# Decoder trunk: two pieces of the second modulation chunk as 128-column products on TensorE, the forget columns fetched from ScalarE's queue, the first weight units asked for sooner

## The reference, cut to what matters

```
cond = silu(c)                                  # 2048 numbers
mod  = cond @ w_mod[l] + b_mod[l]               # 2048 x 12288 weights a layer
sh1, sc1, g1, sh2, sc2, g2 = split(mod, 6)
h    = rms_norm(x, gain) * (1 + sc1) + sh1
proj = h @ w_attn_in                            # q, k, v and eight forget columns
...                                             # attention, output projection, MLP; layer 2 with pooling
```

## Time and profile before

| | us |
|---|---|
| median of 3 executions | 2059.95 (2057.93 to 2060.64) |
| the profiled execution's own time | 2060.63 |
| its span, first to last instruction | 2059.0 |
| TensorE busy in the span | 1987.6 (97%) |
| VectorE busy | 1661.6 (81%) |
| ScalarE busy | 1058.5 (51%) |
| GpSimd busy | 271.1 (13%) |

### The profile page before, as it was taken

How to read it: one execution, slowest core, us unless ns; L and a number is a source line. 1 busy time by engine, 2 the same in 40 slices (tenths; PEclk the granted TensorE clock), 3 DMA queues, 4 the chain that set the end, 5 groups by cost and what they waited for, 6 DMA issues and landing times.

```text
span 2059.0 us, 29840 instructions
## 1 busy us (share of the span) xinstructions
PE 1987.6 (97%) x10792; PEld 1711.1 (83%) x10792; DVE 1661.6 (81%) x2185; ACT 1058.5 (51%) x1556; POOL 271.1 (13%) x459
## 2 busy tenths in 40 slices
PE   3999999998999999999999999899999999999998
PEld 2878989887888888888888887688888888888886
DVE  5777899897899999999989977889965666566665
ACT  4323764554655544565446565565543555434553
POOL 3242342220111111111111100011000000000000
PEclk8999999999999999999999999999999999999999
DMA  9999899896789999998999874397756555555552
GB/s 361 356 357 324 308 333 333 301 321 216 270 311 326 315 375 349 323 331 313 353 367 322 312 260 155 110 321 266 263 193 198 184 187 195 191 191 195 187 185 101
DMA packets 235984, 558.99 MB, mean 271 GB/s; under 512 B 14040, under 2 KB 15048, under 8 KB 235336
## 3 DMA queue, kind: packets, MB, share of 16 engines
q1 hardware_dynamic: 180552, 355.81, 50.0%
q0 software_dynamic: 55296, 201.35, 27.5%
HBM read 555.02 MB, written 2.10 MB: 271 GB/s over the span
## 4 chain that ended last, share of the span: by engine, by line
PE 78%; DVE 10%; issue 5%; DMA 4%; ACT 2%; POOL 0%; DVEq 0%; POOLq 0%; ACTq 0%
PE ps L767 28%; PE ps L772 14%; PE ps L791 8%; PE ps L793 8%; PE ps L792 8%; DVE w_lo L1561 4%; PE ps L811 3%; DMA mraw<-in_w_mod 3%; PE ps L742 2%; PE ps L743 2%; PE ps L744 2%; PE ps L808 1%; DVE macc L1590 1%; DVE macc L1575 1%; ACT work L1186 1%
## 5 line engine op out<-in xcount | busy, mean ns | idle before, releaser
L1186 ACT ACTIVATE w_hi<-raw 128x1024 fp32r<-128x1024 f32 x640 | 670.9, 1057 | 742.1 <-PE ps L767 261.9
L1561 DVE TENSOR_TENSOR w_lo<-raw,w_hi 128x1024 fp32r<-128x1024 f32 x640 | 766.9, 1224 | 273.2 <-ACT w_hi L1186 272.4
L767 PE MATMUL ps<-h_pair,w_hi 128*128 128x512 f32 x2816 | 684.6, 393 | 7.9 <-DVE w_lo L1561 5.9
L767 PEld LDWEIGHTS ps<-h_pair,w_hi 128*128 128x128 f32 x2816 | 515.2, 188 | 115.7 <-issue 16.3
L772 PEld LDWEIGHTS ps<-h_pair,w_lo 128*128 128x128 f32 x2816 | 360.9, 191 | 14.0
L772 PE MATMUL ps<-h_pair,w_lo 128*128 128x256 f32 x2816 | 365.1, 283 | 0.0
L791 PE MATMUL ps<-w_hi,g_hi 128*128 128x512 f32 x832 | 327.5, 394 | 0.8 <-DVE w_lo L1561 0.6
L793 PE MATMUL ps<-w_hi,g_lo 128*128 128x512 f32 x832 | 324.0, 389 | 0.0
L792 PE MATMUL ps<-w_lo,g_hi 128*128 128x512 f32 x832 | 323.8, 389 | 0.0
L1590 DVE SCALAR_TENSOR_TENSOR macc<-mraw,cond,macc 128x1024 f32<-128x1024 f32 x180 | 230.5, 1282 | 29.1 <-DMA mraw<-in_w_mod 21.2
L1575 DVE SCALAR_TENSOR_TENSOR macc<-mraw,cond,macc 128x512 f32<-128x512 f32 x284 | 196.0, 747 | 30.7 <-DMA mraw<-in_w_mod 22.9
(11 more groups left out here) (182 smaller groups left out, 1571.2 us busy)
## 6 DMA issues: line engine op xcount, KB each, us to landing
mraw<-in_w_mod POOLq DMA_DIRECT2D x358, 512.0 KB, 6.3
raw<-in_w_up SPq DMA_DIRECT2D x176, 1024.0 KB, 6.1
raw<-in_w_down SPq DMA_DIRECT2D x88, 1024.0 KB, 5.9
raw<-in_w_attn_in SPq DMA_DIRECT2D x48, 1024.0 KB, 8.9
raw<-in_w_attn_out SPq DMA_DIRECT2D x16, 1024.0 KB, 7.4
work<-in_w_mod POOLq DMA_DIRECT2D x12, 512.0 KB, 8.7
early<-in_w_mod POOLq DMA_DIRECT2D x8, 512.0 KB, 12.5
raw<-in_w_pool SPq DMA_DIRECT2D x4, 1024.0 KB, 5.2
```

The costliest lines, as they stand in the source:

```text
L767: i = mm(ps[:, bank + t, :], w_hi[:, s, kk, t * P:(t + 1) * P], h_pair[:, k, :, :].rearrange("p a t -> p (a t)"), start=first and half == ...
L1186: return nc.scalar.activation(o, i, f, **kw)
L1561: V.tensor_tensor(w_lo[:, s, :, :], raw[:, j % 4, h * 1024:(h + 1) * 1024].rearrange("p (k n) -> p k n", k=2), w_hi[:, s, :, :].bitcast(F3 ...
```

## The change

It has five parts.

1. Pieces 6 and 7 of chunk 1 leave VectorE (4 of its 14 operations). TensorE multiplies them instead (`seed_product`): the piece's 128 x 128 blocks stand still and a column of `cond`, repeated 128 times, moves, so the products both scale the rows and sum them over the partitions. Piece 6 comes first, then the accumulator of VectorE against 128 columns of ones, then piece 7, all into PSUM bank 3. `mod_bias` of chunk 1 reads every 128th column there.
2. SP asks for units 0 to 3 when `mod_acc` reaches 14, 19, 22 and 32. Chunk 1 adds only 10 of its 14 counts by products; the other 4 are added after its last addition.
3. `bfb` is issued by SP right behind the parameters. `wf` is issued by ScalarE, behind the four copies of the first quarter of `h`.
4. TensorE runs `mod_sum` of chunk 0 ahead of the transposes of x, and the transposes of the parameters behind the first two of the eight groups of x. ScalarE copies in that order.
5. VectorE's `mod_bias` of chunk 0 moves behind the last addition of chunk 1; those of chunks 2, 4 and 6 move ahead of the last piece of the chunk that follows.

```diff
@@ -344,6 +344,8 @@
+        SEEDS = (6, 7)
+        X_BANKS = (0, 1, 2, 0, 1, 2, 4, 5)
...
@@ -494,10 +496,13 @@
                     sp.dma_start(prow[0:FT2, CWcol(l, i):CWcol(l, i) + P], rows(conv_w[l, i])).then_inc(s_prm, 16)
                 sp.dma_start(prow[0:FT2, CBcol(l):CBcol(l) + P], rows(conv_b[l])).then_inc(s_prm, 16)
+            with nc.allow_non_contiguous_dma("the forget bias on every partition"):
+                sp.dma_start(bfb[:, :], b_forget[0:1, :].to_broadcast([P, NF])).then_inc(s_wf, 16)
             def load(q, j, src):
                 if isinstance(q, int) and q == 0:
-                    sp.wait_ge(mod_acc, (22, 24, 26, 34)[j])
+                    sp.wait_ge(mod_acc, (14, 19, 22, 32)[j])
                     if j >= 2:
...
@@ -514,11 +519,6 @@
                              src.rearrange("(k p) n -> p k n", p=P)).then_inc(raw_landed[j % 4], 16)
             for pos in range(48):
-                if pos == 4:
-                    with nc.allow_non_contiguous_dma("the eight forget columns, the bias on every partition"):
-                        sp.dma_start(wf[:, :, :], w_attn_in[0, :, 3 * D:3 * D + NF]
-                                     .rearrange("(k p) n -> p k n", p=P)).then_inc(s_wf, 16)
-                        sp.dma_start(bfb[:, :], b_forget[0:1, :].to_broadcast([P, NF])).then_inc(s_wf, 16)
                 hg, kind, ks = qkv_unit(pos)
...
@@ -830,6 +830,26 @@
                            start=True, stop=True)
                 i.then_inc(mod_red, 1)
+            def seed_product(j):
+                pe.wait_ge(early_landed[j], 16)
+                for kk in range(2):
+                    for t in range(4):
+                        i = mm(ps[:, 3, t * P:(t + 1) * P], mod_slot(1, j)[:, kk, t * P:(t + 1) * P],
+                               cond[:, 2 * j + kk:2 * j + kk + 1].to_broadcast([P, P]),
+                               start=j == SEEDS[0] and kk == 0 and t == 0,
+                               stop=j == SEEDS[1] and kk == 1, skip_group_check=True)
+                return i
+            def seeded_sum():
+                seed_product(SEEDS[0])
+                pe.wait_ge(mod_added, 2)
+                for t in range(4):
+                    mm(ps[:, 3, t * P:(t + 1) * P], macc[:, 0, 0, t * P:(t + 1) * P], ones[:, :],
+                       start=False, stop=False, skip_group_check=True)
+                seed_product(SEEDS[1]).then_inc(mod_red, 1)
...
@@ -892,26 +912,35 @@
             pe.wait_ge(consts, C_IDENT)
             pe.wait_ge(s_c, 16)
             nc.tensor.transpose(ps[:, 7, 0:KT], prow[0:KT, 0:P], ident[0:KT, 0:KT]).then_inc(c_t, 1)
-            pe.wait_ge(xn0_ready, 2)
-            for b in range(8):
-                if b >= 4:
-                    pe.wait_ge(x_copied, b - 3)
+            def turn_x(b):
+                if 3 <= b < 6:
+                    pe.wait_ge(x_copied, b - 2)
+                elif b >= 6:
+                    pe.wait_ge(prm_ready, b - 5)
                 for t in range(2):
                     for a in range(QT):
                         k = 2 * b + t
-                        i = nc.tensor.transpose(ps[:, b % 4, (2 * t + a) * P:(2 * t + a + 1) * P],
+                        i = nc.tensor.transpose(ps[:, X_BANKS[b], (2 * t + a) * P:(2 * t + a + 1) * P],
                                                 xn_first[:, a, k * P:(k + 1) * P], ident[:, :])
                 i.then_inc(x_t, 1)
+            pe.wait_ge(consts, C_ONES)
+            pe.wait_ge(cond_s, 1)
+            pe.wait_ge(xn0_ready, 1)
+            mod_sum(0, 1, 0)
+            pe.wait_ge(xn0_ready, 2)
+            turn_x(0)
+            turn_x(1)
             pe.wait_ge(s_prm, 16 * (3 + 5 * LAYERS))
             for b in range(11):
                 i = nc.tensor.transpose(ps[:, 4 + b // 4, (b % 4) * P:(b % 4) * P + ROWS[b]],
                                         prow[0:ROWS[b], b * P:(b + 1) * P], ident[0:ROWS[b], 0:ROWS[b]])
                 if b in (3, 7, 10):
                     i.then_inc(prm_t, 1)
-            pe.wait_ge(prm_ready, 3)
-            pe.wait_ge(consts, C_ONES)
-            pe.wait_ge(cond_s, 1)
-            mod_sum(0, 1, 0)
+            for b in range(2, 8):
+                turn_x(b)
...
@@ -1045,9 +1074,12 @@
                     mod_sum(3, 0, 0)
-            mod_sum(1, 0, 0)
-            pe.wait_ge(x_copied, 8)
+            seeded_sum()
+            pe.wait_ge(x_copied, 6)
+            pe.wait_ge(prm_ready, 3)
             for pos in range(POS0):
+                if pos == 1:
+                    pe.wait_ge(x_copied, 8)
                 start_unit(pos)
...
@@ -1290,6 +1329,10 @@
             for cq in range(3):
                 first_products(2 * cq + 2, 1, 2 * cq + 1)
                 modulate(0, range(4 * cq, 4 * cq + 4))
+                if cq == 0:
+                    with nc.allow_non_contiguous_dma("the eight forget columns"):
+                        act.dma_start(wf[:, :, :], w_attn_in[0, :, 3 * D:3 * D + NF]
+                                      .rearrange("(k p) n -> p k n", p=P)).then_inc(s_wf, 16)
                 if cq < 2:
                     part_copy(6 * cq)
...
@@ -1564,7 +1607,8 @@
             def piece(c_all, j, a):
-                if j:
+                seeded = isinstance(c_all, int) and c_all == 1
+                if j and not (seeded and j in SEEDS):
                     dve.wait_ge(*mod_landing(c_all, j))
                     for kk in range(2):
                         k = 2 * j + kk
@@ -1575,9 +1619,11 @@
                         V.scalar_tensor_tensor(macc[:, a, kk, :], mod_slot(c_all, j)[:, kk, :], cond[:, k:k + 1],
                                                macc[:, a, kk, :], ALU.mult, ALU.add).then_inc(mod_acc, 1)
                 if j == 7:
-                    dve.wait_ge(mod_acc, 14 * since(c_all) + 14)
+                    dve.wait_ge(mod_acc, 14 * since(c_all) + (14 - 2 * len(SEEDS) if seeded else 14))
                     V.tensor_tensor(macc[:, a, 0, :], macc[:, a, 0, :], macc[:, a, 1, :],
                                     ALU.add).then_inc(mod_added, 1)
+                    if seeded:
+                        dve.sem_inc(mod_acc, 2 * len(SEEDS))
...
@@ -1715,8 +1764,10 @@
                         norm_stats(0)
                     if ch == 0 and j == 6:
                         norm_rstd(0)
-                    if ch == 1 and j == 6:
+                    if ch == 1 and j == 7:
                         dve.wait_ge(prm_ready, 3)
+                        mod_bias(ch - 1, 0, first_chunk(ch - 1))
+                    if ch > 1 and ch % 2 and j == 6:
                         mod_bias(ch - 1, 0, first_chunk(ch - 1))
                     if ch >= 2:
                         if ch % 2 == 0 and j == 1:
@@ -1728,8 +1779,6 @@
                             part_add(first + ((0, 6), (1, 2), (1, 5)).index((ch % 2, j)))
                 if ch % 2:
                     cq = ch // 2
-                    if ch > 1:
-                        mod_bias(ch - 1, 0, first_chunk(ch - 1))
                     mod_bias(ch, 0, first_chunk(ch))
                     norm_gain_vec(0, 4 * cq, 4 * cq + 4)
                     for t in range(4 * cq, 4 * cq + 4):
```

More of the change, by code:

```diff
@@ L1265, in _, with x_copy @@
             first_products(1, 0, None)
-            for b in range(8):
+            def x_copy(b):
                 act.wait_ge(x_t, b + 1)
-                A(xnT[:, 2 * b:2 * b + 2, :].rearrange("p a n -> p (a n)"), ps[:, b % 4, :],
+                A(xnT[:, 2 * b:2 * b + 2, :].rearrange("p a n -> p (a n)"), ps[:, X_BANKS[b], :],
                   ACT.Copy).then_inc(x_copied, 1)
+            for b in range(2):
+                x_copy(b)
             for b, (n0, n1) in enumerate(((0, 4), (4, 8), (8, 11))):
@@ L1595, in mod_bias @@
                 dve.wait_ge(mod_red, c_all + 1)
-                V.tensor_tensor(mods[:, ds(4 * c_l + 96 * l, 4)], ps[:, 7, 256:260],
+                sums = ps[:, 7, 256:260]
+                if isinstance(c_all, int) and c_all == 1:
+                    sums = ps[:, 3, :].rearrange("p (t n) -> p t n", t=4)[:, :, 0]
+                V.tensor_tensor(mods[:, ds(4 * c_l + 96 * l, 4)], sums,
                                 prm[:, ds(P * (1 + l) + 4 * c_l, 4)], ALU.add).then_inc(mod_ready, 1)
```

## The result

The changed kernel is slower. Against the kernel before, the ratio of its runs is 1.0027, with a 95% interval of 1.0017 to 1.0036: a median of 2064.1 us against 2058.3. Faster was forecast, 2054.5. One of its eight executions took 3354 us at a mean granted clock of 0.56 and is left out of these numbers. The profiled execution took 2062.49 us, with a span of 2060.9.

A forecast was written before the change was run, and what follows sets the result against it. TensorE, busy 97% of the span with its long waits in the first 44 us, was the bound. Earlier position 0 (-3.8), clock (-2.2) and chunk 3 (+0.5) gave -5.5 us: 2055.1 profiled, 2054.5 median, range 2050.5 to 2066.

The forecast's parts named there:

- rival B: No change, 2058, chance 0.23: low clock delays and slows position 0, or unit 2 and chunk 3 give gains back.
- clock term: Position 0's first 13 passes no longer run at the low clock: 2.2 us won, bounds 0 and 2.7.
- A: Behind position 2, TensorE waits for `wf`, landing at 69.1; position 3 at 74.4, +4.5 us, 2064.5; chance 0.30.
- Both arguments against A: At the `wf` transfer: columns may share SP's queue, where 14.9 us sufficed, or SP may run dry, leaving engines free.
- term for chunk 3: Chunk 2's last piece lands about 3 us later, against time saved at unit 4: 0.5 us charged, bounds 0 and 2.

The follow-up runs named there:

- wf_mid: The changed kernel with the forget columns (`wf`) asked for by ScalarE at 33 us instead of 40.7; ratio 0.9989 to the kernel before.
- wf_sp: The changed kernel with the forget columns asked for by SP between units 3 and 4 again; no wait for them, no lead at position 18.
- wf_first: The changed kernel with the forget columns as ScalarE's first request; ratio 0.9994 to the kernel before.
- wf_mid_again: A second run of wf_mid, unchanged; ratio 0.9982 to the kernel before.
- wf_27: The changed kernel with the forget columns asked for by ScalarE at 28 us; median 3.2 us above that of wf_mid_again.
- moved_only: The kernel before with only `wf` and `bfb` at their new places; columns landed 24.9 us after the ask, ratio's interval holds 1.

## Why the prediction was wrong

Right, by the terms of its own sum:
- Unit 0 landed at 36.06 (forecast 35.7), unit 1 at 43.66 (43.4), unit 2 at 53.07 (51, wanted at 53.58, so it nearly came late). Unit 4 was asked for at 46.87 (near 47).
- Chunk 1's pieces 6 and 7 landed at 33.73 and 35.86 (33.9, 35.9), VectorE was done at 33.8 (34.1), the three groups of products ended at 35.8, 36.7 and 38.5 (35.7, 36.6, 38.4). A pass of width 128 takes 0.11 to 0.12 us there.
- Position 0 began at 39.70 (40.0): 4.1 us won for 3.8. The clock stayed full: 2.74 us won for 2.2. The first half of rival B did not occur.

One reading behind the clock term is weaker than it looks. The granted clock of the earlier trace rows is 1.00 for both stretches of L902, with passes of 0.217 us (3.47 / 16, not 0.213) and of 0.11 under it; in both traces it reads 1.00 without a break from 24 us until the first fall, so that early the step of the clock is seen in the passes alone. By the passes the changed kernel, too, goes over to the fast ones at about 30.4, with transposes on TensorE. So the rule that the Trainium skill states for transposes (TensorE: Matmul & The Clock Gate, Part 4) finds no support in either trace, by the lengths of the passes.

Wrong: the step under "Rivals" that gave A only 0.30, and so left the wait for `wf` out of the sum. The sum had nothing for it; it measured 5.87 us of idle time and 2.5 us of slow products behind it. Its mechanism is what happened: ScalarE's queue takes turns with SP's, packet by packet, as the Trainium skill has it (DMA: Bandwidth & Descriptors, Queues, rings and completion order); the trace agrees, 445 to 444. Both arguments against A fell. The columns do not share SP's queue (they are q10). SP did not run dry in time: it sent 444 packets from 46 to 52 us and 1334 from 52 to 60, and only from then on few, 122 in the 6.5 us up to the landing.

Within A two sizes were off. I had 60 packets a us beside POOL's queue and 170 without it; measured are 74 (445 in 6 us, in which POOL's queue was not full all the time) and 171 (1370 in 8 us). POOL's pause was twice as long as I took it, so 1903 packets had passed by 60 (88 more in 42 to 46). But the last 161 of the 2064 that the queue shows took until 66.4, in which POOL's queue was full again; why these were so slow the trace doesn't show. Landing was 66.4 instead of 69.1, position 3 began at 71.6 and not at 74.4, and the lag there was 1.7 us, not 4.5. That A's 2064.5 is so near to the median of 2064.1 is therefore luck: the trace shows 1.6 to 2.0 us of it.

The term for chunk 3 (0.5, bounds 0 and 2) was too small as well, hidden by the wait in the changed kernel; this is the second half of rival B. Where the wait is gone, as in wf_mid, TensorE waits 1.4 us for unit 4's split and 1.2 us for chunk 3's addition:

```profile
PE ps L742 <- DVE w_lo L1603: 1.4, 1, 1.4
PE ps L829 <- DVE macc L1622: 1.2, 1, 1.2
```

And nothing in my sum looked beyond 84 us. The kernel before asks for chunk 5's sum at 121.36, and in the four profiles of the sooner start that wait there beside wf_sp it can be had at 117.3 to 118.2; so chunk 5 caps the lead at 3.1 to 4.0 us by this estimate, and at 1.1 in wf_sp (120.31). Even with A excluded the forecast gain of 5.5 us was too large: wf_mid gained 2.3 and 3.7 us by its ratios, and the interval of the second just reaches the forecast's 0.9974.

Left open: the median of the changed kernel is 4 to 6 us above that of the kernel before, its profile only 1.6 to 2.0 behind at position 18. The spans of two equal programs differ by up to 2.4 us, but of the variants that have the sooner start and don't wait for the columns, most gain 1 to 4 us less in the ratio than they lead at position 18 (wf_first: lead 3.8, ratio 0.9994, that is 1.2 us); wf_mid_again gains 2 us more. Set side by side by ScalarE's 1394 activations, the profiles say where the rest arises: leads change between 240 and 1300 us, by up to 3.3 us (wf_27: 3.3, then 0.0), and by no more than 0.1 us from there to the end. What changes them there, and what happens in the executions that weren't profiled, no run here shows.

## What to carry to other kernels

A transfer of many tiny packets is priced here by its packets: one turn for each against the other queues with work (835 beside 837 and 757 in wf_mid). Work out its landing from the packet rates of the queues beside it, for the new asking time and the new time of need, before calling a move free; on a queue of its own, beside two busy ones, these columns took 25 to 31 us here. When two edits are made together, ask of each wait that the one hides whether the other uncovers it. And where the DMA engines are full, look for the next place at which the compute engine meets a landing, and for what lets those transfers be asked for: that is how much of a gain at the start can arrive.

## What the runs showed of the hardware

- ScalarE's requests have a queue of their own, q10, which alternates with SP's q1: 883 packets of 32 bytes to 884 of 2 KB in 6 us (moved_only), 445 to 444 in 6 us and 1370 to 1334 in 8 us (the changed kernel).
- Tiny packets in one block on SP's queue pass quickly, 1782 of them in 3 us (wf_sp, 52 to 55 us), and the core moves 239 GB/s meanwhile instead of some 385.
- The same program gets its short spells of low clock (3.4 us each) at different places from one execution to the next: at 78.7 us in wf_mid, at 64.2 and 118.8 in wf_mid_again. Each costs 1.7 us while TensorE is busy, unless a wait behind it takes this up.
